# Second block: the values projected with stationary weights, scaled, and turned back by two transposes behind the first gate chunk

## What is computed

```python
u = rms_norm_2(h, norm_mix[l])
proj = u @ w_in[l]
z_pool, q, k, v, g_pool, g_attn = jnp.split(proj, splits, axis=-1)
y_pool = multiscale_pool(z_pool, w_pool_group[l], pool_scale[l]) @ w_pool_branch[l]
y_attn = windowed_gqa(q, k, v, sink[l]) @ w_attn_branch[l]
merged = jax.nn.sigmoid(g_pool) * y_pool + jax.nn.sigmoid(g_attn) * y_attn
h = h + merged @ w_out[l]
u = rms_norm_2(h, norm_ffn[l])
h = h + (jax.nn.silu(u @ w_ffn_gate[l]) * (u @ w_ffn_up[l])) @ w_ffn_down[l]
```

## Time and profile before

| | us |
|---|---|
| median of 3 runs | 685.66 |
| lowest and highest of them | 683.92, 688.18 |
| span of the profiled execution | 681.9 |
| PE busy | 633.8 (93%) |
| DVE busy | 356.7 (52%) |
| ACT busy | 294.6 (43%) |
| POOL busy | 51.3 (8%) |

### The profile page before, as it was taken

How to read it: one execution, slowest core, us unless ns; L and a number is a source line. 1 busy time by engine, 2 the same in 40 slices (tenths; PEclk the granted TensorE clock), 3 DMA queues, 4 the chain that set the end, 5 groups by cost and what they waited for, 6 DMA issues and landing times.

```text
span 681.9 us, 10213 instructions
## 1 busy us (share of the span) xinstructions
PE 633.8 (93%) x4027; PEld 479.1 (70%) x4027; DVE 356.7 (52%) x689; ACT 294.6 (43%) x562; POOL 51.3 (8%) x76
## 2 busy tenths in 40 slices
PE   8999899998998766879899999999999999999996
PEld 5979788842543320334389999998788888888884
DVE  5687664731031020110188876757856666666665
ACT  6855572431011010100185755564665555555554
POOL 3100101100010000000049000000000000000001
PEclk9999999999999997879999999999999999999999
DMA  8956328999999999999997333355535555555101
GB/s 341 420 227 245 130 118 346 395 382 426 426 389 424 421 420 420 422 421 420 423 420 295 131 125 124 124 186 186 185 128 193 193 195 194 200 194 186 62 1 62
DMA packets 26286, 180.73 MB, mean 265 GB/s; under 512 B 3184, under 2 KB 3312, under 8 KB 5120
## 3 DMA queue, kind: packets, MB, share of 16 engines
q1 hardware_dynamic: 25200, 177.60, 66.1%
q10 hardware_dynamic: 1040, 2.50, 0.9%
HBM read 179.04 MB, written 1.05 MB: 264 GB/s over the span
## 4 chain that ended last, share of the span: by engine, by line
PE 69%; DMA 16%; DVE 8%; ACT 5%; issue 2%; SPq 0%; POOLq 0%; POOL 0%; ACTq 0%; DVEq 0%
PE ps L1612 66%; DMA ring<-stream_dram 15%; PE ps L1615 3%; DVE ring_r L408 3%; ACT single L401 1%; DMA h<-x_dram 1%; DVE work L1547 1%; ACT work L887 1%; DVE work L1550 1%; DVE h L1600 0%; DVE work L1603 0%; ACT turned L892 0%; ACT work_r L883 0%; DVE extra_r L503 0%; DVE work L1428 0%
## 5 line engine op out<-in xcount | busy, mean ns | idle before, releaser
L1612 PE MATMUL ps<-turned,single 128*128 128x256 f32 (+2 forms) x944 | 231.2, 326 | 1.6 <-ACT work L664 0.8
L1612 PE MATMUL ps<-turned,ring_r 128*128 128x256 f32 (+1 forms) x648 | 179.7, 281 | 0.0
L1612 PEld LDWEIGHTS ps<-turned,single 128*128 128x128 f32 x944 | 156.2, 189 | 18.5 <-issue 2.0
L408 DVE TENSOR_TENSOR ring_r<-ring,single 128x1024 fp32r<-128x1024 f32 (+1 forms) x132 | 160.3, 1236 | 14.1 <-ACT single L401 13.9
L401 ACT ACTIVATE single<-ring 128x1024 fp32r<-128x1024 f32 (+1 forms) x132 | 134.0, 1046 | 0.1
L1612 PEld LDWEIGHTS ps<-turned,ring_r 128*128 128x128 f32 x648 | 121.1, 188 | 0.4
L1612 PE MATMUL ps<-ring,work 128*32 128x512 f32 (+2 forms) x462 | 69.9, 611 | 16.0 <-DMA ring<-stream_dram 13.9
L1612 PEld LDWEIGHTS ps<-single 128*128 128x128 f32 x257 | 38.7, 190 | 34.0 <-issue 22.8
L1612 PE MATMUL ps<-single,turned 128*128 128x512 f32 (+3 forms) x208 | 59.2, 364 | 2.4 <-DVE turned L1227 1.5
L1612 PE MATMUL ps<-single 128*128 128x512 f32 (+1 forms) x257 | 55.7, 356 | 2.9 <-DVE single L1439 1.9
L1612 PE MATMUL ps<-single,work_r 128*128 128x512 f32 x176 | 56.2, 392 | 0.0
(11 more groups left out here) (260 smaller groups left out, 719.1 us busy)
## 6 DMA issues: line engine op xcount, KB each, us to landing
ring<-stream_dram SPq DMA_DIRECT2D x145, 1024.0 KB, 12.4
work<-stream_dram SPq DMA_DIRECT2D x12, 1024.0 KB, 12.5
turned_w<-stream_dram SPq DMA_DIRECT2D x4, 1024.0 KB, 14.4
extra<-stream_dram SPq DMA_DIRECT2D x2, 1024.0 KB, 11.4
ring<-stream_dram SPq DMA_DIRECT2D x2, 832.0 KB, 8.4
h<-x_dram SPq DMA_DIRECT2D x2, 512.0 KB, 4.9
gain<-gains_dram ACTq DMA_DIRECT2D x2, 512.0 KB, 10.4
yields<-stream_dram SPq DMA_DIRECT2D x1, 1024.0 KB, 13.0
```

The lines of the kernel that those rows point to most:

```text
L408: dve.tensor_tensor(ring_r[:, place, a], ring[:, place, a], w_hi[k % HIGHS][:, a].bitcast(F32), ALU.subtract).then_inc(s["wlo_done"], 1)
L1612: return pe.matmul(o, lhsT, rhs, start=start, stop=stop, **kw)
```

## The change

The values are now computed by `chunk` like `k`: 24 matmuls, weights stationary, all 256 tokens moving, into bank 6. DVE multiplies the result by `row2` into `vT`, a tile of 128 x 256 that uses memory of `pt2`. Two transposes on PE, behind the first gate chunk of the loop, turn it into bank 7, and `values_out` on ACT copies it in two instructions of 128 x 256, without a factor. The 24 matmuls of `values(1)`, which stood between the first two score products and the first gate chunk, are gone.

```diff
+        vT = pt2[:, 1, :]
...
             def values_out():
-                act.wait_ge(s["v2_ps"], 1)
-                for i in range(NT):
-                    for j in (0, 2):
-                        last = act.activation(v2[:, i, :].rearrange("p (a j b) -> p a j b", j=3, b=HD)[:, :, j, :],
-                                              ps[:, 6, i * P:(i + 1) * P].rearrange("p (a b) -> p a b", b=HD), ACT.Copy,
-                                              scale=rsd[:, i:i + 1])
+                act.wait_ge(s["v2_ps"], 2)
+                for j in (0, 2):
+                    last = act.activation(v2.rearrange("p i (a j b) -> p i a j b", j=3, b=HD)[:, :, :, j, :],
+                                          ps[:, 7, 0:TOK].rearrange("p (i a b) -> p i a b", a=2, b=HD), ACT.Copy)
...
             k2_low(dve, 0)
+            dve.wait_ge(s["v2_ps"], 1)
+            dve.tensor_tensor(vT, ps[:, 6, 0:TOK], row2, ALU.mult).then_inc(s["vt_sb"], 1)
             split_low(dve, SPLIT1 + 5)
...
-            def values(i):
-                for t in range(DT):
-                    begin, last = triple(ps[:, 6, i * P:(i + 1) * P], [u[:, t, i * P:(i + 1) * P] for u in (u_hi, u_lo)],
-                                         [w[:, D + t * P:D + (t + 1) * P] for w in split_pair(SPLIT1 + 4)], t == 0, t == DT - 1)
-                return last
-
-            split_ready(SPLIT1 + 4, 1)
             pe.wait_ge(s["q2_sb"], 3)
-            values(0)
+            chunk(ps[:, 6, 0:TOK], SPLIT1 + 4, 1, (u_hi, u_lo)).then_inc(s["v2_ps"], 1)
+
+            def turn_values():
+                pe.wait_ge(s["vt_sb"], 1)
+                for i in range(NT):
+                    last = turn(ps[:, 7, i * P:(i + 1) * P], vT[:, i * P:(i + 1) * P])
+                last.then_inc(s["v2_ps"], 1)
...
             scores2(0)
             scores2(1)
-            values(1).then_inc(s["v2_ps"], 1)
...
+                if u == 0:
+                    turn_values()
```

More of the change, by code:

```diff
@@ L324, in two_blocks @@
             yp_ps yp_sb s2_ps nm2_done e2_done p2_done pt2_ps pt2_sb o2_ps o2_sb sig_done br_ps br_sb
-            mg_done h3_ps h3_done f_ps fsg_done fh_sum fh_high fh_done facc_ps whi_done wlo_done o2_low yp_low mg_sum mg_high att_low cm_ps cm_sb sqs_done h4_done hg_done y_done y_left""".split()
+            mg_done h3_ps h3_done f_ps fsg_done fh_sum fh_high fh_done facc_ps whi_done wlo_done o2_low yp_low mg_sum mg_high att_low vt_sb cm_ps cm_sb sqs_done h4_done hg_done y_done y_left""".split()
         s = {n: sem(n) for n in names}
```

## The result

The changed kernel takes 686.61 us (median of 20 runs) against 684.38 us for the kernel before (20 runs). The ratio is 1.0029, with a 95% interval of 1.002 to 1.0038. By the ratio it is 2.0 us slower (the two medians differ by 2.2 us), and the interval is clear of no change. The profiled execution has a span of 684.8 us, against 681.9.

The account below looks back on a forecast made before the run. The chain of DVE and ACT up to PE's transposes of u = 1 was taken as the bound. Its 1.2 us plus 1.3 us for the clock gave 2.5 us, so 688.2 us from 685.66; range 684.8 to 690.2 us.

Parts of the forecast that it names:

- PE's own work: Values on PE: 24 wide matmuls replace 48 narrow, 2.86 for 5.24 us; with two transposes, about 2.2 us less.
- The prediction's comparison with an isolated product: Values' matmuls by the skill page's isolated figures: 2.7 us narrow against 2.6 us wide, so PE would save nothing.
- Steps 1 to 3: From the values' chunk to gate chunk 0: values' scaling starts at 376.91, 0.44 us long; PE then idles 1.1 us.
- Steps 4 to 6: Gate chunk, value transposes, ACT's copies: copies start 1.64 us later, take 0.56 for 1.02 us; net delay 1.2 us.
- Steps 7 and 8: Up to PE's transposes of u = 1: they start 1.2 us later, at 388.2, after PE idles about 2.8 us.
- The clock: At PE's 2.8 us wait: the clock more likely than not falls to 0.50, costing 1.3 us, bounds 0 and 4.6.
- the sum of two idle times in the expert stage: Two PE waits of 1.43 and 1.42 us, together 2.85 us, preceded half clock there; used as ground for a fall.
- The forecast's case: Around PE's transposes of u = 1: chain 1.2 us longer and clock loss 1.3 us, giving 688.2 us; chance 50%.
- the rival "the clock holds": At PE's new wait: chain 1.2 us longer but no clock fall, giving 686.9 us; chance 30%.
- No later stage takes up the delay: Behind the transposes of u = 1: order and durations stay as before, so the 1.2 us chain delay reaches the end.
- "faster, since PE's work was on the path": At ACT's value copies: if not late, PE's saved 2.2 us would count, at best 683.5 us; chance 7%.
- "It moves nothing": Between ACT's value copies and the transposes of u = 1: the 1.2 us delay melts, giving 685.7 us; chance 8%.

Follow-up runs that it names:

- e6_after_reordered: Changed kernel with ACT copying the values later and DVE making one low half after normalising u = 1; 683.14 us, ratio 0.9972.
- e4_all: Changed kernel with values scaled between the two gate halves, ACT's value copies later, one DVE low half after normalising u = 1; 682.74 us, ratio 0.9971.
- e5_before_reordered: Kernel before, narrow matmuls kept, with ACT copying the values later and DVE making one low half after normalising u = 1; 684.72 us, ratio 0.9992.
- e1_turn_first: Changed kernel with the transposes of the scaled values ahead of the first gate chunk; 683.76 us, ratio 0.999.
- e8_look_2: Changed kernel unaltered, second of three further profiled executions to see whether the clock falls; it falls; no median or ratio given.
- e3_scale_later: Changed kernel with DVE scaling the values between the two low halves of the first gate slot; 687.05 us, ratio 1.0038.

## Why the prediction was right, point by point

The forecast was 688.2 us, made on a median of 685.66 us for three runs. Over 20 runs the kernel before has a median of 684.38 us, so the same +2.5 us would stand at 686.9, and 686.61 was measured. The three runs had been 1.3 us too high. Taken as absolute times, 686.61 is therefore nearer to the rival's 686.9 than to the forecast's 688.2; the forecast is to be judged by the difference, 2.5 us against 2.0 us by the ratio and 2.2 us by the medians.

- **PE's own work.** Forecast 2.86 us for the wide matmuls and 2.2 us less in all. The trace has them from 374.09 on at the same 0.119 us each, and PE's busy time over A and B is 1.96 us less where the clock holds. Once nothing hides the gain it is 1.3 to 1.5 us (e6_after_reordered and e4_all against e5_before_reordered), less than 2.2 us. PE now idles ahead of gate chunk 0 (0.46 us in e4_all, 0.90 us in e6_after_reordered, against 0.27 us ahead of the scores in e5), and in e4_all DVE's normalisation ends just behind PE's own work; the rest of the difference was not traced. The prediction's comparison with an isolated product was no measure for this stream, in which each matmul has a weight load of its own (4027 of each in the kernel before); nothing in the sum rested on it.
- **Steps 1 to 3.** The scaling starts 377.14 - 374.29 = 2.85 us behind that of `k`, forecast 376.91 - 374.05 = 2.86 us. The idle time ahead of gate chunk 0 is 0.89 us, forecast 1.1 us: I counted from 377.46, where the next matmul had started, and not from the end of the scores' last one, some 0.2 us later.
- **Steps 4 to 6.** ACT's copies start 382.13 - 374.29 = 7.84 us behind the scaling of `k`, forecast 381.92 - 374.05 = 7.87 us, and hold ACT for 0.54 us, forecast 0.56 us.
- **Steps 7 and 8.** A is 1.12 us longer, forecast 1.2 us; the idle time is 2.74 us, forecast 2.8 us.
- **The clock.** Taken as more likely than not, at 1.3 us. It fell in three of five executions and cost 1.44 to 1.50 us where it did, since it fell near the end of the idle time and nearly the whole stretch lay in work: the upper value of the forecast, 0.45 x 3.3. The ground that I gave for it, the sum of two idle times in the expert stage, was not tested; that the chance came out near what was forecast is in part luck. The forecast's case and the rival "the clock holds" are both true, each of a part of the executions, and the median lies between them. The prediction put them as cases that exclude each other; an average over both, with the share of 0.6 that is known only now, 1.2 + 0.6 x 1.3 = 2.0 us, is nearer to the 2.0 us measured.
- **No later stage takes up the delay.** B differs from before by the clock's term alone (by 0.03 us at most where the clock holds), and A + B is 2.62 us longer where the span is 684.8 - 681.9 = 2.9 us longer; the scaling of `k` itself was 0.24 us later in that execution.

Of the rivals, "faster, since PE's work was on the path" would have needed what e4_all adds: ACT and DVE out of the way. "It moves nothing" is what e1_turn_first comes to, by moving two transposes.

## What to carry to other kernels

Before you save work on the busiest engine, read which engine the chain is on while that work runs: here PE worked in the shadow of 12.97 us of DVE and ACT, so 2 us less work on PE became idle time. A result that is finished sooner helps only if its consumer is not queued behind something longer; place the step that hands it on (here the transposes) in the wait that opens, not behind the next long piece of work. And when work turns into one long wait, add the clock to the bill, as a chance and not as a certainty.

## What the runs showed of the hardware

- One idle time of PE of 2.74 us between dense fp32r matmuls let the granted clock fall to 0.50 in three of five executions of the same program, and did not in two. With 2.62 us (e3_scale_later) it fell in the one execution seen. With 1.78 and 1.76 us it did not in two. The stretch at 0.50 lasted about 3.4 us each time, and the loss was 1.44 to 1.50 us by B. It began between 0.3 us ahead of the end of the idle time (e8_look_2) and 1.2 us behind it (e3_scale_later), so the cause can stand a microsecond ahead of the first slow matmul. The Trainium skill (page "TensorE: Matmul & The Clock Gate", section "HAM oscillation — how this bites in real kernels") describes this for waits on a DMA of about 3 to 5 us; these runs show it for a shorter wait, on VectorE, and that the same gap may or may not do it.
- fp32r matmuls with 128 moving columns are 0.109 us apart and those with 256 columns 0.119 us, each with its own weight load, so half the columns save 8% of the time.
- ScalarE's copy from PSUM of 128 x 256 without a factor holds it for 0.27 us (0.54 us for two), that of 128 x 128 with a factor per partition for 0.255 us (1.02 us for four, in the kernel before). Two of the first in place of four of the second hold ScalarE 0.48 us less; how much of that the factor makes was not tried.
